# Eight gate units as seven quarter products each, the late modulation under attention, and branch sums on GpSimd

## What is computed

```python
h = rmsnorm(x, g_pre_mix) * (1 + scale1) + shift1           # shift, scale, gate from silu(cond) @ w_ada
(na_q, na_k, na_v, m_q, m_k, m_v, m_o, m_i, m_f,
 cv_b, cv_c, cv_x, gate_pre) = split(h @ w_in)
att = neighborhood_attention(...)                           # 8 heads x 64; context tokens: plain attention
hm  = bidir_mlstm(...)                                      # 4 heads x 128, chunks of 128 tokens
hm  = hm * rsqrt(mean(hm * hm) + EPS) * m_norm_g * sigmoid(m_o)
hc  = cv_b * short_conv(cv_c * cv_x, conv_w)
g   = sigmoid(gate_pre + b_gate)                            # three gates of 1024 columns
merged = g[0] * (att @ w_br_na) + g[1] * (hm @ w_br_m) + g[2] * (hc @ w_br_cv)
x  = x + gate1 * rmsnorm(merged @ w_out, g_post_mix)
h2 = rmsnorm(x, g_pre_ffn) * (1 + scale2) + shift2
x  = x + gate2 * rmsnorm((silu(h2 @ w_ffn_gate) * (h2 @ w_ffn_up)) @ w_ffn_down, g_post_ffn)
```

## Time and profile before

| | |
|---|---|
| median of three runs | 1138.51 us |
| the profiled execution | 1139.12 us, its span 1137.2 us |
| granted TensorE clock, mean | 0.999 |
| PE busy | 1119.5 us, 7324 matmuls |
| DVE busy | 724.0 us |
| ACT busy | 477.5 us |
| POOL busy | 70.5 us |
| moved by DMA | 130.22 MB, 115 GB/s |

### The profile page before, as it was taken

The page is one execution under the profiler, slowest core; times in us unless marked ns, Lnnn a source line. Parts: engine busy times, 40 slices in busy tenths (PEclk is TensorE's granted clock), DMA queues, the critical chain, the costliest instruction groups (busy, mean ns, idle before and its releaser), DMA issues.

```text
span 1137.2 us, 18483 instructions
## 1 busy us (share of the span) xinstructions
PE 1119.5 (98%) x7324; PEld 1058.7 (93%) x7324; DVE 724.0 (64%) x1297; ACT 477.5 (42%) x881; POOL 70.5 (6%) x123
## 2 busy tenths in 40 slices
PE   6999999999999999999999999999999999999997
PEld 4799999899999999999999988999999999988886
DVE  5734545458575655687885446899897777633444
ACT  5534444344333343322222338655555555533431
POOL 2051101000000000400000002000000000000002
PEclk9999999999999999999999999999999999999999
DMA  9675221132621112345653235143332242325112
GB/s 366 235 218 128 72 76 43 34 111 80 75 70 56 56 58 96 108 130 186 201 186 115 83 121 169 55 167 130 114 110 75 75 148 76 113 66 192 56 37 93
DMA packets 40150, 130.22 MB, mean 115 GB/s; under 512 B 8736, under 2 KB 10304, under 8 KB 38528
## 3 DMA queue, kind: packets, MB, share of 16 engines
q1 hardware_dynamic: 36592, 121.41, 33.1%
q0 software_dynamic: 3472, 7.62, 2.4%
HBM read 121.64 MB, written 7.36 MB: 113 GB/s over the span
## 4 chain that ended last, share of the span: by engine, by line
PE 92%; DVE 4%; ACT 1%; issue 1%; DMA 1%; SPq 0%; POOL 0%; POOLq 0%; ACTq 0%; DVEq 0%
PE ps L2120 28%; PE ps L2122 28%; PE ps L2121 28%; PE ps L2367 1%; PE ps L2382 1%; PE ps L2341 1%; PE ps L2429 1%; PE ps L2431 1%; PE ps L2433 1%; DMA xt<-in_x_sample 1%; PE ps L2308 0%; PE ps L2167 0%; PE ps L2417 0%; DVE w_lo L1502 0%; PE ps L2415 0%
## 5 line engine op out<-in xcount | busy, mean ns | idle before, releaser
L2122 PE MATMUL ps<-h_hi,w_lo 128*128 128x320 f32 x1184 | 365.9, 309 | 0.0
L2120 PE MATMUL ps<-h_hi,w_hi 128*128 128x320 f32 x1024 | 321.3, 314 | 0.2 <-DVE w_hi L1627 0.2
L2121 PE MATMUL ps<-h_lo,w_hi 128*128 128x320 f32 x1024 | 316.4, 309 | 0.0
L2122 PEld LDWEIGHTS ps<-h_hi,w_lo 128*128 128x128 f32 x1184 | 222.2, 188 | 0.0
L1502 DVE TENSOR_TENSOR w_lo<-raw,w_hi 128x1024 fp32r<-128x1024 f32 x109 | 132.7, 1227 | 111.7 <-ACT w_hi L1122 111.0
L2120 PEld LDWEIGHTS ps<-h_hi,w_hi 128*128 128x128 f32 x1024 | 192.4, 188 | 1.9 <-issue 1.2
L2121 PEld LDWEIGHTS ps<-h_lo,w_hi 128*128 128x128 f32 x1024 | 192.4, 188 | 0.1
L2120 PE MATMUL ps<-w_hi,h_hi 128*128 128x512 f32 x378 | 148.7, 393 | 0.0
L2122 PE MATMUL ps<-w_hi,h_lo 128*128 128x512 f32 x378 | 147.2, 389 | 0.0
L2121 PE MATMUL ps<-w_lo,h_hi 128*128 128x512 f32 x378 | 147.2, 389 | 0.0
L1122 ACT ACTIVATE w_hi<-raw 128x1024 fp32r<-128x1024 f32 x109 | 113.3, 1052 | 32.2 <-PE ps L2122 31.4
(11 more groups left out here) (284 smaller groups left out, 1823.3 us busy)
## 6 DMA issues: line engine op xcount, KB each, us to landing
raw<-in_w_blocks SPq DMA_DIRECT2D x182, 512.0 KB, 3.8
ada<-in_w_first SPq DMA_DIRECT2D x8, 1024.0 KB, 20.2
xline<-x SPq DMA_DIRECT2D x5, 512.0 KB, 5.1
x<-xline SPq DMA_DIRECT2D x5, 512.0 KB, 7.6
xt<-in_x_sample SPq DMA_DIRECT2D x4, 512.0 KB, 6.5
condr<-in_cond_rows POOLq DMA_DIRECT2D x2, 1024.0 KB, 7.8
vtok<-vline POOLq DMA_DIRECT2D x8, 256.0 KB, 9.4
g<-gline SPq DMA_DIRECT2D x2, 1024.0 KB, 6.7
```

The lines of the kernel that those rows point to most:

```text
L2120: nc.tensor.matmul(dst, wh, xh, start=first, stop=False, skip_group_check=resumed)
L2121: nc.tensor.matmul(dst, wh, xl, start=False, stop=False, skip_group_check=resumed)
L2122: return nc.tensor.matmul(dst, wl, xh, start=False, stop=last, skip_group_check=resumed)
```

## The change

- Gates b = 0 and 1 are eight wide units (`NG = 8`), 84 matmuls each, numbered in front of those of the feed-forward, which become `NG` to `WT - 1`. They stand in one stretch behind mo. For them POOL rebuilds h from `h_hi` and `h_lo` (`reb`), DVE makes the four sums (`gsum`), ACT and DVE split them (`gsplit`).
- Each unit's tanh goes to a staging tile, is stored to DRAM (`gdram`) and loaded again (`gload`) for the branch unit that needs it.
- The eight branch units of b = 0 and 1 follow behind the last gate unit, one after the other. DVE's drain keeps the multiplication; the sum into `merged` is an instruction of POOL.
- Chunks 0 to 3 of the mLSTM norm stand inside the gate units, chunk 4 at the first two groups of the first branch unit. The splits of att stand in the last gate unit (`att_split`), those of the mLSTM output in the second branch unit (`hm_split`).
- The 24 late modulation blocks stand among the weight blocks of k, q, mq, mk and mv. They use a copy of the condition rows of their own, `condr_a`, loaded by POOL and put through SiLU by ACT at the first use of k.
- V for the latent pairs is loaded by POOL pair by pair (`values`) instead of whole; the key cache is loaded by POOL instead of SP.

```diff
-ADA_AHEAD, ADA_PER_GATE = 2, {2: (0, 0, 0, 0), 0: (1, 4, 4, 4), 1: (4, 4, 1, 0)}
+NG = 8
...
+    for i in range(4):
+        u += [("gate", (2, i), KD, UW), ("br", (2, i), 4, UW)]
+    u += [("mo", 0, KD, UW), ("mo", 1, KD, UW)]
+    u += [("br", (b, i), 4, UW) for b in range(2) for i in range(4)]
...
+def adas_behind(kind, which, p):
+
+    if kind == "mv":
+        return 4 if p == 3 else 0
+    if (kind, which) == ("mk", 1):
+        return 2 if p == 0 else 0
+    if kind in ("q", "k", "mq", "mk") and (kind, which) != ("q", 0):
+        return 1 + p
+    return 0
...
+    def gate_stretch():
+
+        g0, d0 = BLOCK_OF[UNIT_OF[("mo", 0)], 0], BLOCK_OF[UNIT_OF[("br", (0, 0))], 0]
+        behind = {0: [("ada_turn", 2), ("ada_store", 2)],
+                  1: [("wsum", 0), ("wop", 0, 0), ("wop", 0, 1)],
+                  2: [("gsum", 0)],
+                  3: [("gsum", 1), ("gsum", 2), ("gsplit", 0), ("wop", 0, 2), ("wop", 0, 3)],
+                  4: [("gsplit", 1), ("gsum", 3)],
+                  5: [("gsplit", 2), ("wop", 0, 4), ("wop", 0, 5)],
+                  7: [("gsplit", 3)]}
+        plan.append(("reb",))
+        for j in range(8):
+            m, f, h = j // 4, j // 2 % 2, j % 2
+            if h == 0:
+                plan.append(("use", g0 + j // 2))
+            if j == 0:
+                split_to(g0 + 4)
+            group("mo", UNIT_OF[("mo", m)], f, h)
+            plan.extend(behind.get(j, []))
+        for w in range(NG):
+            c = w // 2
+            for q in range(7):
+                plan.append(("wu", w, q))
+                if q == 2:
+                    plan.append(("hm", w % 2, c))
+                if q == 4 and w % 2:
+                    plan.append(("hm", 2, c))
+                if w >= 2 and q == 2:
+                    plan.append(("gload", w - 2)) if w == 2 else None
+                if w == NG - 1:
+                    if q in (1, 3, 5, 6):
+                        split_to(d0 + (1, 3, 5, 6).index(q) + 1)
+                    if q in (3, 5):
+                        plan.append(("att_split", q // 2 - 1))
+        plan.append(("gates_end",))
+        plan.append(("gload", 1))
+        for u in range(8):
+            n = UNIT_OF[("br", divmod(u, 4))]
+            b = BLOCK_OF[n, 0]
+            for j, emit in enumerate(tiles(n)):
+                if j == 0:
+                    plan.append(("use", b))
+                if j == (0 if u < 7 else 2):
+                    split_to(b + BLOCKS_HELD)
+                if u == 0 and j < 2:
+                    plan.extend([("hm", 0, 4)] if j == 0 else [("hm", 1, 4), ("hm", 2, 4)])
+                if (u, j) == (1, 0):
+                    plan.append(("hm_split",))
...
+                if j == 1 and 1 <= u < 7:
+                    plan.append(("gload", u + 1))
+                emit()
...
+                elif step[0] == "reb":
+
+                    pool.wait_ge(ml_h, len(ML_UNITS))
+                    pool.wait_ge(merged_add, 16)
+                    for dst, k0, h in ((tq12, 0, 1), (tq22, 4, 1), (tq11, 0, 0), (tq21, 4, 0)):
+                        nc.gpsimd.tensor_tensor(dst[:, :, :], h_hi[:, k0:k0 + 4, half(h)].bitcast(F32),
+                                                h_lo[:, k0:k0 + 4, half(h)].bitcast(F32),
+                                                ALU.add).then_inc(reb_done, 1)
...
+                    nc.gpsimd.tensor_tensor(mg, mg, (gt, gt2)[i % 2][:, f, half(h)], ALU.add).then_inc(merged_add, 1)
...
+                elif B0 <= b < B0 + BLOCKS_HELD:
+                    act.wait_ge(fp_done, 7 * (NG - 1) + (2, 4, 6, 7)[b - B0])
...
+                    if UNITS[n][:2] == ("k", 0) and part == 0:
+                        act.wait_ge(condr_in, 32)
+                        nc.scalar.activation(condr_a[:, :, :], condr_a[:, :, :], ACT.Silu).then_inc(condr_rd, 1)
...
                 if adas_done(b) == 1:
-                    dve.wait_ge(condr_rd, 1)
+                    dve.wait_ge(condr_rd, 2)
...
-                    else:
-                        nc.vector.tensor_tensor(mg, mg, v, ALU.add).then_inc(merged_add, 1)
...
+                if w == 0 and q == 0:
+                    pe.wait_ge(act_drain, drains("A", gid("mo", 1, 1, 1)))
```

More of the change, by code:

```diff
@@ L97, in weight_units @@
             u.append(("down", (c, i), DOWN_TILES[i], 512))
+    u += [("ada", (m, j), KD, P) for m in (2, 4, 3) for j in range(KD)]
     return u
@@ L117, in parts_of, with block_order @@
     return 0 if kind == "mif" else kc * w // 1024
-BLOCKS = [(n, p) for n in range(len(UNITS)) for p in range(parts_of(n))]
+def adas_behind(kind, which, p):
[6 more added lines that the diff above has]
+    return 0
+def block_order():
+    late = [n for n in range(FIRST_ADA, len(UNITS)) if UNITS[n][0] == "ada"]
+    order = []
+    for n in range(len(UNITS)):
+        if UNITS[n][0] != "ada":
+            for p in range(parts_of(n)):
+                order.append((n, p))
+                order += [(late.pop(0), 0) for _ in range(adas_behind(*UNITS[n][:2], p))]
+    assert not late
+    return order
+BLOCKS = block_order()
 BLOCK_OF = {np_: b for b, np_ in enumerate(BLOCKS)}
@@ L216, in unit @@
             later = 0
[L217 to L230, removed]
-                else:
-                    split_to(BLOCK_OF[n, 0] + j)
-            elif j % 2 == 0 and j // 2 < parts_of(n):
+            if j % 2 == 0 and j // 2 < parts_of(n):
                 plan.append(("use", BLOCK_OF[n, j // 2]))
@@ L367, in make_plan @@
                 side += [[("ml", 0, s)], [("ml", 1, s)]]
[L368 to L371, removed]
-        if kind == "mo" and which == 1:
-            for c in range(TT + 2):
-                side.append([("hm", 1, c)] * (c < TT) + [("hm", 2, c - 2)] * (c >= 2))
         n += 1
@@ L560, in place @@
                            cb=C_CB)[kind] + which * UW + part * P
-WU_PLACES = [place("fg" if w % 2 == 0 else "fu", 1 + w // 2, f) for w in range(WU) for f in range(2)]
+WU_PLACES = [place("gate", divmod(w, 4), f) for w in range(NG) for f in range(2)] + [place("fg" if w % 2 == 0 else "fu", 1 + w // 2, f) for w in range(WU) for f in range(2)]
 ADA5_PLACES = [place("ada", (5, j), 0) for j in range(KD)]
@@ L1709, in wide_unit @@
                         operand_lo(1, 0)
+                elif q in (2, 3, 4):
+                    if more:
+                        operand_lo(w + 1, q - 1)
+                elif q == 5:
+                    if more:
+                        operand_lo(w + 1, 4)
+                    gate_collect(w, 1)
+                else:
+                    gate_collect(w, 2)
+                    if more:
+                        operand_lo(w + 1, 5)
+            def wide_unit(w, q):
+                more = w + 1 < WT
+                if q == 0:
+                    if w % 2 == 0 and w > NG:
+                        collect(w - 1, 3)
+                    operand_lo(w, 6)
+                    if more and w > NG:
+                        weight_sums(w + 1)
+                elif q == 1:
+                    if more and w > NG:
+                        operand_lo(w + 1, 0)
+                    collect(w, 0)
+                    if w == NG:
+                        weight_sums(w + 1)
+                        operand_lo(w + 1, 0)
                 elif q == 2:
@@ L2160, in group @@
                     bank_free(g)
+                if kind == "br" and which == (0, 0):
+                    pe.wait_ge(gate_tanh, 4 * (NG - 1))
+                    pe.wait_ge(fz, NG - 1)
+                    pe.wait_ge(fy, NG - 1)
+                    pe.wait_ge(hm_out, 3)
                 if kind == "ada_row":
```

497 lines of the change are left out of this document (323 added, 174 removed).

## The result

The changed kernel takes 1147.4 us (median of 4 runs, 1146.7 to 1148.0), the kernel before 1138.55 beside it (4 runs): ratio 1.0077, 95% interval 1.006 to 1.0095. It is 8.9 us slower, where I had forecast 1.9 and had let the range end at 1146.5. The profiled span grew from 1137.2 to 1145.9 us, by 8.7.

A forecast was written before the change was run, and what follows sets the result against it. TensorE (PE), busy 98% of the span, was taken as the bound; -14.0 + 0.7 + 3.5 + 9.9 + 1.8 = +1.9 us on the 1137.2 us span, so a median of 1140.4 us, range 1133.5 to 1146.5.

The forecast's parts named there:

- The products: Gate units: 84 matmuls instead of 96 in each of eight units saves 96 matmuls of 0.1456 us, -14.0 us.
- POOL rebuilds h behind the mo groups: Start of the gate stretch: four POOL adds of some 3.7 us end before the mo stage; nothing, 3 us if they double.
- the start's +0.7: Start of the gate stretch: the first product waits for the last mo drain and semaphores, +0.7 us (0.4 to 1.5).
- Between gates and branches: First branch unit: PE stops for chunk 4's norm, so its second group starts +9.9 us late (6 to 11.5).
- The clock, +1.8: Behind the gate-to-branch gap: PE resumes at 1.2 GHz and 3.7 us do half their work, +1.8 us (0 to 3.7).
- Attention, +3.5: Under attention: late modulation blocks on DVE make PE wait, mainly at pairs 1 and 2, +3.5 us together (1 to 9).
- the 0.4 at k's second block: Start of k: modulation waits for ACT's SiLU, so the remainder of k's second block comes late, +0.4 us.
- the 0.2 at pair 7: Attention pair 7: three hi halves stand ahead of the copy of the probabilities, +0.2 us.
- Branch sums on POOL: Branch units: four POOL adds take at most 6.8 of a unit's 7.0 us, so nothing; bound 1 us.
- B: Rival: chunk 4's chain hides, gate-to-branch place costs 4, clock stays, attention 2; 1131.2 us, partly so 1132 to 1136; chance 0.22.
- D: Rival: gate units' quarter products are fed too late and save nothing, +14.0, 1154.4 us; chance 0.03.
- C: Rival: DVE saturates under attention at the normalisation of pairs 3 to 6, +5.6, 1146.0 us; chance 0.25.

The follow-up runs named there:

- experiment 1: Changed kernel with the four adds that rebuild h moved from POOL's queue to DVE's, nothing else changed: 1140.8 us, ratio 1.0017.
- experiment 3: Changed kernel with the output norm of token chunk 4 moved from the first branch unit into the last two gate units: 1139.4 us, ratio 1.0005.
- experiment 4: Changed kernel with each late modulation chunk multiplied and summed over 512 of its 1024 elements, part of the computation left out: 1144.1 us, ratio 1.0048.
- experiment 7: Changed kernel with POOL's four adds copying only the high part (one SBUF input), part of the computation left out: 1140.9 us, ratio 1.0019.
- experiment 2: Changed kernel with the third gate operand's splitting issued behind the last mo group instead of the sixth, adds still on POOL: 1143.0 us, ratio 1.0042.

## Why the prediction was wrong, by its steps

- **The products, -14.0 us: right.** PE count 7228, 345 matmuls in 50 us.
- **The step that failed: "POOL rebuilds h behind the mo groups ... Taken at nothing", and with it the start's +0.7.** It measured +6.9, and experiment 1, which changes the engine of those adds alone, brought 6.3 of it back and left a wait of 0.62. I asked only when POOL would be done, and there I was near: 3.7 us per add forecast, 3.41 measured (2.96 for the one that did not wait for DVE). I did not ask what a POOL instruction does to DVE. While POOL ran the four adds DVE got one instruction through for each, so DVE lost 3.90 + 3.46 + 3.35 + 3.34 less their own 1.21 + 3 x 0.69, 10.8 us, at the one place where the next operands hung on it. My outer bound of 3 us was for POOL being late, the wrong engine. The Trainium skill, "SBUF — State Buffer", section "SBUF: two separate sides", has the rule: VectorE and GpSimd share one pair of ports under an exclusive lock for a whole instruction, and a VectorE instruction with two SBUF inputs is blocked while a GpSimd one that reads SBUF runs. The traces agree with that rule, with 3.41 beside 3.34 to 3.46, 1.70 beside 1.63 to 1.74 and 1.31 beside 1.26 to 1.37 us. It would have shown four DVE instructions of 3.4 us ahead of time.
- The kernel before already showed it, behind a mean. The earlier trace rows has 726 ns for POOL's one-input scaling of mo, which I took as what such an instruction costs, without asking what it waits for. One by one, three of the eight are:

```profile
457.40 0.46 POOL L1073 TENSOR_SCALAR mo<-mo 128x320 f32<-128x320 f32 x1 [3.06 <-ACT mo L1219]
...
472.26 1.12 POOL L1073 TENSOR_SCALAR mo<-mo 128x320 f32<-128x320 f32 x1
...
480.18 1.45 POOL L1073 TENSOR_SCALAR mo<-mo 128x320 f32<-128x320 f32 x1
```

  The first fell into 12.9 us in which DVE stood idle; beside the second DVE had a two-input remainder from 471.84 to 473.06, of its usual 1.22 us, so here it was POOL that waited. The same instruction took 0.46 us alone and up to three times that beside DVE.
- **Between gates and branches: right, +9.9 us forecast and 9.9 measured.** The first branch group started at 584.75 and PE resumed with the transposes at 596.39, 11.64 us later where the forecast had 11.65; less the group's own 1.75 that is 9.9. The waits of 2.6 and 6.1 us are 8.7 of it; most of the rest is the end of the first group, already at 1.2 GHz. Experiment 3 confirms the chain.
- **The clock, +1.8: too small.** The gap cost 12.4 in all, so 2.5 are left for the clock behind it. It had fallen behind the short wait already, at 588.7, and came back 5.9 us after PE resumed and not 3.7. Another 1.5 went at the gate start, which hangs on the failed step.
- **Attention, +3.5: right in the sum**, 3.2 measured and 3.2 taken back by experiment 4, **but not in its parts.** The waits stood ahead of the transposes of pairs 1 (0.28 + 0.29 us, 1.2 forecast) and 2 (1.08, 1.7 forecast); pair 0 waited too, 0.60, where I had none, and the 0.4 at k's second block and the 0.2 at pair 7 did not come. That the sum fits so well is in part luck.
- **Branch sums on POOL: right at nothing.** Most POOL adds took 0.88 us and PE had no wait there. There too POOL and DVE take turns: the add begun at 613.59, beside a DVE remainder until 614.71, took 1.86. But a short instruction beside a half-idle DVE delays nobody that PE waits for.
- With the failed step undone and all else left, the kernel took 1140.8 us, against the 1140.4 forecast; with attention's parts and the clock as above, so near a hit is luck too. Rivals B and D fell. C's number came nearest (1146.0), but its mechanism did not happen: pairs 3 to 7 had no wait.

## What to carry to other kernels

Before moving an elementwise operation to POOL, look at what DVE does in the same microseconds: a DVE instruction with two SBUF inputs that starts beside a long POOL instruction waits for its end, and here 5.96 us of work on DVE was cheaper than 13.6 us on the "free" engine. Where an engine's queue is in program order, put work that can be late behind drains that PE needs, not ahead of them. Waits that a change brings can each be small and removable: with three of them removed the same idea gave 1131.3 us, 0.65% under the kernel before.

## What the runs showed of the hardware that was not expected

- POOL is held off as well as DVE: sixteen short adds took 20.9 us where four long ones took 13.6, and the one-input scaling of mo 0.46 us alone and 1.12 to 1.45 beside DVE. What an instruction takes when it does not wait shows in the first of each series, which began before DVE's: 2.96 us for a 1280-element add (the others 3.42 to 3.94), 1.27 for the one-input form of experiment 7 (mean 1.70) and 0.87 for a 320-element add (1.33 beside the sums).
- A DVE instruction that has only one input in SBUF, the other being a bank of PE's results, was not held off. The changed kernel's POOL, then its DVE, in the branches: the drain lies inside POOL's add and takes the 0.49 us that it takes elsewhere.

```profile
615.42 0.87 POOL L1191 TENSOR_TENSOR merged<-merged,gt 128x320 f32<-128x320 f32 x1
```

```profile
615.67 0.49 DVE L1797 SCALAR_TENSOR_TENSOR gt<-gt,ps 128x320 f32<-128x320 f32 x1 [0.51 <-PE ps L2375]
```

- Waits of nearly the same length did not do the same to the clock: 2.20 us inside gate unit 0 (experiment 2) left it at 1.00, 2.16 us at the first branch unit (experiment 3), behind a short run of transposes, was followed by 0.51. The changed kernel's 2.59 us at the same place, without transposes just ahead, was followed by 0.50 too, so the transposes alone do not tell them apart. Nor does a longer wait fix the moment: in the wait of 5.22 us ahead of the first product the clock fell only as PE resumed, at 482.9, in the changed kernel, and in experiment 3 some 3 us before PE resumed, in a wait of the same 5.22 us. What decides it stays open.
- The clock at 1.2 GHz lasted for some 3.4 us of work after the 5.2 us wait, 3.4 us after the 2.2 us wait of experiment 3 and 5.9 us after the 6.1 us wait.
